# Branch and mixing weights of an encoder layer as half chunks in four shared slots

## The reference, cut to what matters

```python
merged = g_attn * (attn @ w_attn_o) + g_rec * (rec @ w_lru_o)   # the branches
x = x + merged @ w_out                                          # the mixing
x = x + moe(rmsnorm(x))                                         # 32 experts, top 4
# each expert: w_gu (1024 x 2048) and w_down (1024 x 1024), 12.6 MB; 402.7 MB in all
```

## Time and profile before

| what | before |
|---|---|
| median of 3 runs | 1137.63 us |
| span of the profiled execution | 1134.2 us |
| around the span, by the median | 3.4 us |
| TensorE matmul busy | 1084.8 us, 96% |
| DMA rate over the span | 388 GB/s |
| share of the chain that ended last | PE 67%, DMA 28% |

### The profile page before, as it was taken

The page is one execution under the profiler, slowest core; times in us unless marked ns, Lnnn a source line. Parts: engine busy times, 40 slices in busy tenths (PEclk is TensorE's granted clock), DMA queues, the critical chain, the costliest instruction groups (busy, mean ns, idle before and its releaser), DMA issues.

```text
span 1134.2 us, 12887 instructions
## 1 busy us (share of the span) xinstructions
PE 1084.8 (96%) x5407; PEld 503.4 (44%) x5407; DVE 371.1 (33%) x645; ACT 237.2 (21%) x369; POOL 2.6 (0%) x10
## 2 busy tenths in 40 slices
PE   7999999999999999999998989898989899899987
PEld 7999899633333333333333333333333333333332
DVE  6997887522212222122121211111211212121212
ACT  5399961211111111111111110011110101010102
POOL 0000000000000000000000000000000000000000
PEclk9999999899999999999999999999999999999999
DMA  9544277999999999999999999999999999999996
GB/s 353 185 178 149 84 287 300 419 425 399 431 425 428 426 434 432 433 426 435 431 429 436 430 430 436 429 430 436 430 432 433 429 436 430 427 427 429 426 428 247
DMA packets 25637, 439.77 MB, mean 388 GB/s; under 512 B 3425, under 2 KB 4065, under 8 KB 6273
## 3 DMA queue, kind: packets, MB, share of 16 engines
q1 hardware_dynamic: 24976, 438.27, 91.5%
q10 hardware_dynamic: 624, 0.99, 0.2%
HBM read 438.20 MB, written 1.05 MB: 387 GB/s over the span
## 4 chain that ended last, share of the span: by engine, by line
PE 67%; DMA 28%; DVE 2%; SPq 1%; ACT 1%; issue 0%; DVEq 0%
PE ps L1491 26%; DMA slots<-in_w_down_dram 22%; PE ps L1500 13%; PE ps L1172 13%; DMA slots<-in_w_gu_dram 5%; PE ps L1455 5%; PE ps L1436 3%; PE ps L1549 2%; DVE slots_r L725 1%; SPq L403 1%; PE ps L1229 1%; PE ps L1450 1%; PE ps L1414 1%; PE ps L1234 0%; PE ps L1526 0%; PE ps L1274 0%
## 5 line engine op out<-in xcount | busy, mean ns | idle before, releaser
L1500 PE MATMUL ps<-slots,lru 128*64 128x512 f32 x1024 | 239.8, 610 | 17.2 <-DMA slots<-in_w_down_dram 17.2
L1491 PE MATMUL ps<-slots,lru 128*64 128x512 f32 x1024 | 227.7, 594 | 11.7 <-DMA slots<-in_w_gu_dram 11.2
L1491 PE MATMUL ps<-slots,qT 128*64 128x512 f32 x984 | 223.8, 596 | 4.6 <-DMA slots<-in_w_gu_dram 4.6
L1491 PEld LDWEIGHTS ps<-slots,lru 128*64 128x64 f32 x1024 | 74.1, 137 | 160.8 <-issue 139.7
L1491 PEld LDWEIGHTS ps<-slots,qT 128*64 128x64 f32 x984 | 68.9, 137 | 152.2 <-issue 144.8
L1500 PEld LDWEIGHTS ps<-slots,lru 128*64 128x64 f32 x1024 | 68.5, 139 | 142.5 <-issue 123.5
L1100 DVE COPY lru<-ps 128x512 f32<-128x512 f32 x32 | 22.1, 692 | 322.9 <-PE ps L1491 322.9
L1172 PE MATMUL ps<-slots_r 128*128 128x256 f32 (+1 forms) x812 | 107.7, 291 | 0.2 <-DVE slots_r L725 0.2
L1172 PEld LDWEIGHTS ps<-slots_r 128*128 128x128 f32 x812 | 102.2, 191 | 5.4 <-issue 2.5
L653 ACT ACTIVATE lru<-ps 128x512 f32<-128x512 f32 x32 | 19.1, 598 | 395.3 <-PE ps L1491 395.3
L1082 DVE TENSOR_SCALAR lru<-sq,rank_col,small 128x64 f32<-128x64 f32 x64 | 17.2, 312 | 241.8 <-PE ps L1436 241.8
(11 more groups left out here) (200 smaller groups left out, 649.3 us busy)
## 6 DMA issues: line engine op xcount, KB each, us to landing
slots<-in_w_gu_dram SPq DMA_DIRECT2D x40, 4096.0 KB, 29.2
slots<-in_w_gu_dram SPq DMA_DIRECT2D x44, 2048.0 KB, 18.9
slots<-in_w_down_dram SPq DMA_DIRECT2D x20, 4096.0 KB, 28.4
slots<-in_w_down_dram SPq DMA_DIRECT2D x22, 2048.0 KB, 20.8
slots<-in_pre_dram SPq DMA_DIRECT2D x13, 2048.0 KB, 8.2
slots<-in_w_down_dram SPq DMA_DIRECT2D x8, 512.0 KB, 31.0
slots<-in_pre_dram SPq DMA_DIRECT2D x3, 1024.0 KB, 6.9
slots<-in_w_gu_dram SPq DMA_DIRECT2D x3, 1024.0 KB, 17.4
```

The source lines that it names most:

```text
L1491: ins = nc.tensor.matmul(ps[64 * side:64 * side + 64, 4 + b, :], xgT[i % 2][:, k, :], rows[r][:, o:o + BANK], start=(k == 0), stop=(k == K ...
L1500: ins = nc.tensor.matmul(ps[64 * side:64 * side + 64, bank, :], actT[(i - 1) % 2][:, k, :], w[:, r, side * BANK:(side + 1) * BANK], start= ...
```

## The change

The chunks 10 to 14 are loaded, split and used as ten halves ("units") of 128 x 2048 floats. A unit's floats land in the first half of a slot; the high part is put in the second half, the low part over the floats, so a unit needs one slot and not two. The units go through slots 2, 3, 4 and 5 in turn. Units 0 to 5 are the branch weights, units 6 to 9 the mixing weights. Slots 0, 1, 6, 7 and the buffer `late` are no longer used by them, and expert chunks are loaded there first; slots 4 and 5 follow after mix(1) and mix(3), slots 2 and 3 after the last `mix_end`. On TensorE mix(0) comes after all eight branch groups. On DVE the low part of unit g+2 follows merge(g) for g from 2 to 6. The core of the diff:

```diff
-        SLOT_ORDER = [2, 3, LOWS, SLOTS - 1, 0, 1, 4, 5]
-        FREED = {2: [(branch_ps, 3)], 0: [(mixed_ps, 1)], LOWS: [(branch_ps, KD)], 4: [(mixed_ps, 2)]}
+        SLOT_ORDER = [0, 1, LOWS, SLOTS - 1, 4, 5, 2, 3]
+        FREED = {4: [(mixed_ps, 1)], 5: [(mixed_ps, 2)], 2: [(mixed_ps, 3)]}
...
+        UNITS = [(10, 0), (10, 1), (11, 0), (11, 1), (13, 0), (13, 1), (12, 0), (12, 1), (14, 0), (14, 1)]
+        UNIT_SLOT = [2, 3, 4, 5, 2, 3, 4, 5, 2, 3]
+        MIX_UNIT = 6
+        UNIT_FREED = [(group_done, 24), (group_done, 24), (group_done, 28), (group_done, 28), (branch_ps, 2),
+                      (branch_ps, 3), (branch_ps, 4), (branch_ps, 6), (branch_ps, 7), (branch_ps, 8)]
...
# SP, before: c is the chunk
-                if c == 13:
-                    sp.wait_ge(group_done, 32)
-                    sp.wait_ge(gate_ps, 32)
-                elif c == 14:
-                    sp.wait_ge(pv_ps, NQ // 2)
-                    half_load(extra_rows(1, 0), EXTRA[1], 0, extra_full[1])
-                    half_load(wide[:, 0:2048], 3, 0, slot_full[SLOTS - 1])
-                    for k in range(2):
-                        expert_load(k)
-                    sp.wait_ge(branch_ps, 6)
...
-            expert_load(2)
-            half_load(wide[:, 2048:], 3, 1, slot_full[SLOTS - 1])
+            for u in range(4):
+                unit_load(u)
+            sp.wait_ge(rec_ok, 2)
+            sp.wait_ge(pv_ps, NQ // 2)
             n, j = step_of(EXTRA[0])
             sp.dma_start(late[:, :], expert_src(n, j)).then_inc(extra_full[0], 16)
-            for k in (4, 5):
-                expert_load(k)
+            half_load(extra_rows(1, 0), EXTRA[1], 0, extra_full[1])
+            sp.wait_ge(group_done, 32)
+            sp.wait_ge(gate_ps, 32)
+            half_load(wide[:, 0:2048], 3, 0, slot_full[SLOTS - 1])
+            expert_load(0)
+            expert_load(2)
+            unit_load(4)
+            unit_load(5)
+            expert_load(1)
+            for u in range(6, 10):
+                unit_load(u)
+            half_load(wide[:, 2048:], 3, 1, slot_full[SLOTS - 1])
             sp.wait_ge(merged_ok, KD)
             half_load(extra_rows(1, 1), EXTRA[1], 1, extra_full[1])
-            for k in RING_CHUNKS[6:SLOTS]:
+            for k in RING_CHUNKS[4:SLOTS]:
                 expert_load(k)
...
# ACT
-            for c in range(12, PRE):
-                split_high(c)
+            for u in range(4, len(UNITS)):
+                unit_split_high(u)
...
# DVE
+            def unit_split_low(u):
+                dve.wait_ge(*unit_high_ok(u))
+                low_part(unit_low(u), unit_whole(u), unit_high(u)).then_inc(split_lo, 1)
...
-                if g == 1:
-                    split_low(12)
-                if g == 3:
-                    split_low(13)
-                if g == KD - 1:
-                    split_low_by_halves(14)
+                if 2 <= g < KD - 1:
+                    unit_split_low(g + 2)
+            unit_split_low(9)
...
# TensorE
+                product(half(4 + g % 2, 1), recurrent, ahead=((unit_high_ok(u),), (unit_low_ok(u),), ()))
...
-            for g in range(4):
+            for g in range(KD):
                 branches(g)
-            mix(0)
-            for g in range(4, KD):
-                branches(g)
-            for c in range(1, 4):
+            for c in range(4):
                 mix(c)
```

More of the change, by code:

```diff
@@ L41 @@
 PAIRS = 3
-PRE = 15
 PER = 6
@@ L271, in casts_before @@
             return 2 * sum(b not in CAST_V for b in range(c))
-        WIDTH = [KD * 2 * KVW if c == Q_CHUNK + 1 else CH for c in range(PRE)]
-        PLACE = [2 * (c % PAIRS) for c in range(PRE - 2)] + [LOWS, 4]
+        WIDTH = [KD * 2 * KVW if c == Q_CHUNK + 1 else CH for c in range(CHUNKS)]
+        PLACE = [2 * (c % PAIRS) for c in range(CHUNKS)]
         def low(c):
@@ L280, in high, with unit_whole, unit_low, unit_high @@
         def high(c):
-            return (late_r if PLACE[c] == LOWS else ring_r[PLACE[c] + 1])[:, 0:WIDTH[c]]
+            return ring_r[PLACE[c] + 1][:, 0:WIDTH[c]]
+        def unit_whole(u):
+            return ring[UNIT_SLOT[u]][:, 0:UNIT]
+        def unit_low(u):
+            return ring_r[UNIT_SLOT[u]][:, 0:UNIT]
+        def unit_high(u):
+            return ring_r[UNIT_SLOT[u]][:, UNIT:]
+        def unit_landed(u):
+            s = UNIT_SLOT[u]
+            return slot_full[s], 16 * (PLACE.count(s) + UNIT_SLOT[:u + 1].count(s))
+        def unit_high_ok(u):
+            return split_hi, casts_before(CHUNKS) + u + 1
+        def unit_low_ok(u):
+            return split_lo, CHUNKS + u + 1
         def whole(c):
@@ L324, in half_load, with unit_load @@
                 sp.dma_start(dst, expert_src(n, j)[:, r * 2048:(r + 1) * 2048]).then_inc(full, 16)
[L326 to L337 removed]
+            def unit_load(u):
+                c, h = UNITS[u]
+                sp.wait_ge(*UNIT_FREED[u])
+                sp.dma_start(unit_whole(u), pre[c, :, h * UNIT:(h + 1) * UNIT]).then_inc(slot_full[UNIT_SLOT[u]], 16)
+            for c in range(1, CHUNKS):
+                if c >= PAIRS:
                     sp.wait_ge(*CONSUMED[c - PAIRS])
@@ L441, in split_high, with unit_split_high @@
                                          ACT.Copy).then_inc(split_hi, 1)
+            def unit_split_high(u):
+                act.wait_ge(*unit_landed(u))
+                nc.scalar.activation(unit_high(u), unit_whole(u), ACT.Copy).then_inc(split_hi, 1)
             def group(i):
@@ L1314, in _, with unit @@
                     values(VALUES_AT.index(i))
-            BLOCKS = CH // P
-            w_br = [chunk(c, BLOCKS) for c in BR_CHUNK]
+            BLOCKS = UNIT // P
+            def unit(u, k):
+                return [b.rearrange("p (k n) -> p k n", k=k) for b in (unit_high(u), unit_low(u))]
+            w_br = [unit(u, BLOCKS) for u in range(MIX_UNIT)]
             def branches(g):
                 first = 12 * g
-                for i, c in enumerate(BR_CHUNK[:2]):
-                    if g > 0 and first <= BLOCKS * i < first + 12:
-                        chunk_in(c)
                 if g >= 2:
@@ L1339, in branches @@
                     pe.wait_ge(group_read, 32)
[L1340 to L1344, removed]
+                product(half(4 + g % 2, 1), recurrent, ahead=((unit_high_ok(u),), (unit_low_ok(u),), ()))
+                u = (first + 11) // BLOCKS
+                product(half(4 + g % 2, 0), attention, ahead=((unit_high_ok(u),), (unit_low_ok(u),), ())
+                        ).then_inc(branch_ps, 1)
             def mix_bank(n, c):
-                w = chunk(MIX_CHUNK[c // 4], 4)
+                w = unit(MIX_UNIT + c // 2, 2)
                 toks, o = slice(n // 2 * P, (n // 2 + 1) * P), (n % 2) * BANK
                 return product(ps[:, n, :], [((merged_hi[:, c, toks], merged_lo[:, c, toks]),
-                                              [b[:, c % 4, o:o + BANK] for b in w])],
+                                              [b[:, c % 2, o:o + BANK] for b in w])],
                                start=(c == 0), stop=(c == KD - 1))
             def mix(c):
-                if c == 0:
-                    chunk_in(MIX_CHUNK[0])
+                if c % 2 == 0:
+                    pe.wait_ge(*unit_low_ok(MIX_UNIT + c // 2))
                 pe.wait_ge(merged_ok, c + 1)
@@ L1363, in mix_end @@
                 for c in range(4, KD):
+                    if n == 0 and c % 2 == 0:
+                        pe.wait_ge(*unit_low_ok(MIX_UNIT + c // 2))
                     pe.wait_ge(merged_ok, c + 1)
```

31 lines of the change are left out of this document (15 added, 16 removed).

## The result

The changed kernel is slower, by 5.3 us where 5.9 were forecast, and through the wait forecast.

A forecast was written before the change was run, and what follows sets the result against it. Bytes set the end after 300 us, the stream waiting on TensorE's releases. branches(7) 6.6 us late, less 0.77, made 5.9: span 1134.2 to 1140.1, median 1137.63 to 1143.5; range 1139.5 to 1147.

The forecast's parts named there:

- The late unit: SP's queue: unit 4, behind expert loads served in order at 2.47 us per MB, lands at 173.7 us.
- The estimate of some 10 us more for three 1 MB loads: SP's queue: by the skill's figures, three 1 MB loads would add some 10 us; the `pbuf` half was said to disagree.
- DVE in front of it: Branch stage: DVE stands 7 us before unit 4's low part, merge(3) behind it; TensorE idles 4.9 us, branches(5) at 180.0.
- Clock and second wait: Branch group 7: unit 6 holds it until 190.4; the lowered clock costs 1.6 us, giving 190.2; the two don't add.
- the third rival: More waits, chance 0.15: each wait lowers the clock again, units 6 and 9 come later; 1147 us.
- From the last mixing to the release: Last mixing to first expert refill: branches(7) 6.6 us late less 0.77 gives 5.9 us, carried to the end.
- Full rooms, and the end: Expert stream: earlier fetches end in full rooms and an idle queue; each microsecond on TensorE's way is one at the end.
- Around the span: Whole kernel: 3.4 us around the span, taking the span of 1140.1 us to a median of 1143.5.
- No wait: Rival, chance 0.12: unit 4 lands before 169 us, DVE never waits, 0.77 us are won; 1136.9 us.
- Faster: Rival, chance 0.05: dips behind refills are load-order gaps that full rooms close; 2.1 us won, 1135.2 with a third dip.
- The range: Median: the forecast's own range 1140.8 to 1146 (chance 0.68), called bounds of unit 4's landing; overall 1139.5 to 1147.
- the late bound: Unit 4's landing in SP's queue: 175.5 us, at the half `pbuf` chunk's price of 2.71 us per MB.

The follow-up runs named there:

- run with the expert loads last: Changed kernel with every expert load moved behind unit 9 in SP's queue; 1147.73 us against 1137.19 for the kernel before, ratio 1.0089.
- run with the merge first: Changed kernel with DVE's low parts one merge later, unit 4's after merge(3), loads as they were; 1139.16 us, ratio 1.0013 to the kernel before.
- filled wait: Changed kernel with 30 transposes into an unused bank ahead of branches(5); 1143.07 us, ratio 1.0054 to the kernel before.
- run with the units first: Changed kernel with units 4 to 6 ahead of the last two expert chunks in SP's queue; 1137.72 us against 1137.41 for the kernel before.
- run with both orders: Changed kernel with units 4 to 6 earlier in SP's queue and DVE's low parts one merge later; 1136.62 us against 1137.19 before, ratio 0.9995.
- half releases: Changed kernel with SP's units earlier, DVE's low parts one merge later, and ten refills issued as halves; 1135.78 us against 1137.19 before.

## Why the prediction was right, point by point

**The late unit.** Forecast: unit 4 lands at 173.7 us, by the price of 2.47 us per MB in a queue served in order. ACT began its cast at 173.83. The order in the queue is shown by the run that moved the units ahead: same loads, no loss. That the forecast came within 0.2 us is luck in part: by the same price unit 4 was to land at 168.5 in that run, and it was cast at 169.99 (16.10 us after the first group, 169.6 on the clock of the kernel before). The estimate of some 10 us more for three 1 MB loads, which the prediction took from the Trainium skill (DMA: Bandwidth & Descriptors, section Bandwidth; its table is for loads issued from GpSimd), isn't borne out for SP's loads: with the halves kept nothing was lost, and in the run with the expert loads last, unit 4, issued at 162.56 on an empty queue, landed in 5.1 us.

**DVE in front of it.** Forecast: 7 us idle, merge(3) behind it, `branches(5)` at 180.0, TensorE idle 4.9 us. Measured: 7.08, 180.03, 4.74. The run with the merge first shows the split of this wait, 1.5 us for the landing and the rest for the order on DVE.

**Clock and second wait.** Forecast: group 7 at 190.4 by unit 6, or 190.2 by the clock, not both. Measured: 190.28, without a wait in front, so it was the clock. Group 5 took 185.96 - 180.03 = 5.93 us instead of 4.32, so 1.6 us for the lower clock, as forecast. The filled wait shows that the two claims don't add.

**What the third rival had.** It took each wait to lower the clock again. The trace of the changed kernel has one fall in this stage, behind 4.74 us without a product. Waits of 1.46 and 0.91 us in the filled run, 1.05 in the run with the merge first and 0.55 in that with the units first were followed by 16 products in 2.17 to 2.18 us, or 8 in 1.22: full speed. Nor did unit 6 come later than forecast: ACT began its cast at 183.68, and the forecast had it land at 184.1.

**From the last mixing to the release.** Forecast: 5.9 us late at the last mixing and unchanged from there. Measured: 205.6 - 199.86 = 5.7 at the last mixing, but 5.10 at the first refill. The step that failed is the one that took the router's stage as a constant. Its two gathers, 1.98 us each in the kernel before, at half the clock, took 1.08 in the changed kernel, where the clock fell later:

```profile
223.47 1.08 PE L1461 MATMUL ps<-hn,lru 128*64 128x512 f32 x4
225.54 0.19 PE L1433 MATMUL ps<-lru,tri 128*128 128x32 bf16 x1 [1.00 <-DVE lru L1039]
...
226.66 1.08 PE L1461 MATMUL ps<-hn,lru 128*64 128x512 f32 x4 [0.85 <-DVE lru L1047]
...
229.48 1.03 PE L1475 MATMUL ps<-sq,qT 128*128 128x128 f32 x4
```

The first gather's 0.9 us were no gain, since TensorE then waited 1.00 us for DVE. The second gather and the product behind it brought 1.0 us, and against that stand 0.4 us more for the transposes of the last line (1.03 us where it was 0.62) and those behind them: 0.6 in all. The sum had no term for what the clock does in that stage.

**Full rooms, and the end.** Forecast: weights fetched earlier end in full rooms and an idle queue, and a microsecond on TensorE's way is one at the end. The idle queue is there (8 GB/s from 234 to 236). For later releases the rule held. For earlier ones ("one less is one less") it isn't shown: 1.34 us of earlier release brought 0.6, with an interval that takes in 1.34 and 0. Earlier loads beyond full rooms only made the queue idle ahead of the first refill: 224 to 230 us ran at 239 GB/s in the run with both orders, 321 with half releases, where the kernel before has no gap (406 and 455 GB/s from 224 to 228).

**Around the span.** The 3.4 us were wrong for a profiled execution, 1.8 is what a run with its own time shows. The span forecast, 1140.1, was low for that reason, and since the profiled execution was the longest of its four; the median, 1143.5, wasn't.

**The rivals.** *No wait* would have needed a landing before 169 us; the run with the units first, at 169.99, was just short of it and had 0.55 us of wait. *Faster* needed gaps that full rooms close; in the run with both orders, where unit 4 was in time, no such gain shows (0.9986 to 1.0004), and the dip behind the release is still there, 299 GB/s from 272 to 274 us, just after the refill of 271.26.

**The range.** The prediction calls 1140.8 to 1146 the bounds of unit 4's landing. Its rows give about 1146 for the late bound, but for the early one only some 1142; the lower end has no working.

## What to carry to other kernels

A prefetch that is moved ahead in a queue served in order delays every later load of that queue by its bytes: before moving it, list which small load comes behind it and who waits for that. A wait placed in an engine's program for data it may not yet have holds back all that stands behind it, so put what others wait for first; here that alone was worth two thirds of the loss. Once the queue runs empty and waits for releases, more prefetch buys nothing. What is left then is to release earlier, which with half releases was worth 0.04 to 0.22% here, or more rooms, which no run tried.

## What the runs showed of the hardware that was not expected

A second queue is no express lane: with both queues at work, the 16 engines together moved 33 packets of SP's and 34 of ACT's in 2 us, but 0.52 MB against 0.28, since the packets of the units were half as long. The first packet of ACT's queue came only 3.4 and 3.5 us after the issue. The first half chunk on its own queue was ready 1.2 us later than in the common one (21.48 and 21.47 us after the first branch group against 20.30).

Work that computes nothing can pay for half of itself: 40 transposes, 4.57 us, in the router's stage delayed the first refill by 2.29 us only. The granted clock stayed up, so that the two gathers behind them took 1.08 us each instead of 1.98, and DVE's work for the second gather was done meanwhile; without this last, as in the changed kernel, the first gather's time stands again as a wait of 1.00 us.
